# Eight heads' sample products of an mLSTM core placed on four column groups of TensorE, with their rows on 128 partitions

## What is computed

```python
S = jnp.einsum('bhtd,bhsd->bhts', qc, kc) * jnp.exp(D - mt[..., None])
wi = jnp.exp(inter - mt)
num = wi[..., None] * jnp.einsum('bhvd,bhtd->bhtv', C, qc) + jnp.einsum('bhts,bhsv->bhtv', S, vc)
den = wi * jnp.einsum('bhd,bhtd->bht', n, qc) + jnp.sum(S, axis=-1)
hc = num / jnp.maximum(jnp.abs(den), jnp.exp(-mt))[..., None]
```

## Time and profile before

| | |
|---|---|
| time, median of 3 runs | 2181.82 us (2179.68 to 2181.86) |
| the profiled execution: its own time | 2179.15 us |
| its span in the trace | 2177.4 us |
| TensorE busy | 2141.7 us, 98% |
| VectorE, ScalarE, GpSimd busy | 59%, 29%, 12% |
| mLSTM stages and output projection | 1352 to 1536 us of the span |

### The profile page before, as it was taken

How to read it: one execution, slowest core, us unless ns; L and a number is a source line. 1 busy time by engine, 2 the same in 40 slices (tenths; PEclk the granted TensorE clock), 3 DMA queues, 4 the chain that set the end, 5 groups by cost and what they waited for, 6 DMA issues and landing times.

```text
span 2177.4 us, 30006 instructions
## 1 busy us (share of the span) xinstructions
PE 2141.7 (98%) x11026; PEld 1680.8 (77%) x11026; DVE 1275.3 (59%) x2997; ACT 641.5 (29%) x1467; POOL 264.1 (12%) x499
## 2 busy tenths in 40 slices
PE   8999999999999999999999999999999999999998
PEld 7656777776878888888888775778888888888887
DVE  5215996654386776777422665443876776676223
ACT  3005885543232222221001220542322222220002
POOL 1002000000012222221000000320122222220000
PEclk9999999999999999999999999999999999999999
DMA  8135405984312232221222224132322222222223
GB/s 198 55 96 163 132 2 140 268 213 104 101 39 78 87 98 87 78 78 59 97 78 78 88 78 98 59 100 70 114 83 78 78 78 78 78 88 86 78 78 113
DMA packets 206916, 209.66 MB, mean 96 GB/s; under 512 B 40467, under 2 KB 192251, under 8 KB 206515
## 3 DMA queue, kind: packets, MB, share of 16 engines
q1 hardware_dynamic: 202754, 189.99, 30.5%
q0 software_dynamic: 4016, 17.75, 2.4%
HBM read 196.33 MB, written 19.70 MB: 99 GB/s over the span
## 4 chain that ended last, share of the span: by engine, by line
PE 95%; DVE 2%; ACT 1%; issue 1%; DMA 0%; SPq 0%; DVEq 0%; ACTq 0%
PE PS L2824 57%; PE PS L2685 4%; PE PS L768 3%; PE PS L1630 3%; PE PS L1770 2%; PE PS L2670 2%; PE PS L1525 2%; PE PS L1569 2%; PE PS L2784 2%; PE PS L697 2%; PE PS L684 2%; PE PS L717 2%; PE PS L2599 1%; PE PS L756 1%; PE PS L782 1%; PE PS L889 1%
## 5 line engine op out<-in xcount | busy, mean ns | idle before, releaser
L2824 PE MATMUL PS<-HT,ring 128*128 128x272 f32 x1536 | 374.3, 393 | 4.0 <-DVE HT L3534 4.0
L2824 PEld LDWEIGHTS PS<-HT,ring 128*128 128x128 f32 x1536 | 291.9, 190 | 65.2 <-issue 3.6
L2824 PE MATMUL PS<-arena,ring 128*128 128x272 f32 x1392 | 341.8, 392 | 0.0
L2824 PEld LDWEIGHTS PS<-arena,ring 128*128 128x128 f32 x1392 | 264.3, 190 | 54.4
L3168 ACT ACTIVATE arena<-arena,CB,CW 128x560 f32<-128x560 f32 x128 | 109.0, 853 | 377.5 <-DVE arena L3594 313.2
L2824 PE MATMUL PS<-arena,CONST 128*128 128x272 f32 x768 | 191.7, 392 | 0.0
L2824 PE MATMUL PS<-arena 128*128 128x272 f32 x768 | 191.3, 392 | 0.0
L3609 DVE SCALAR_TENSOR_TENSOR arena<-arena,CW 128x560 f32<-128x560 f32 x256 | 187.3, 790 | 0.0
L2824 PEld LDWEIGHTS PS<-arena,CONST 128*128 128x128 f32 x768 | 145.9, 190 | 30.1
L2824 PEld LDWEIGHTS PS<-arena 128*128 128x128 f32 x768 | 145.8, 190 | 30.0
L3808 POOL COPY arena<-arena 128x16 f32<-128x16 f32 x128 | 50.9, 398 | 622.9 <-DVE arena L3594 525.2
(11 more groups left out here) (517 smaller groups left out, 3359.8 us busy)
## 6 DMA issues: line engine op xcount, KB each, us to landing
ring<-in_w_ffn_up SPq DMA_DIRECT2D x64, 1024.0 KB, 6.5
ring<-in_w_ffn_down SPq DMA_DIRECT2D x32, 1024.0 KB, 5.1
ring<-in_cache_nsa_kv SPq DMA_DIRECT2D x128, 128.0 KB, 6.0
arena<-in_cache_nsa_kv SPq DMA_DIRECT2D x56, 256.0 KB, 6.4
ring<-in_w_ml_in SPq DMA_DIRECT2D x12, 1024.0 KB, 5.9
arena<-in_cache_nsa_win SPq DMA_DIRECT2D x16, 512.0 KB, 5.6
out_nsa_win_sample<-in_cache_nsa_win POOLq DMA_DIRECT2D x8, 1016.0 KB, 17.5
ring<-in_w_nsa_in SPq DMA_DIRECT2D x6, 1024.0 KB, 5.4
```

Source lines behind the costliest of these rows:

```text
L2824: last = mm(PS[:, bank, 0:HALF], lhs[:, k, :], rhs(k), start=(first and k == 0), stop=(done and k == 3))
```

## The change

In all of it head h = 4r + j gets the column group j (PSUM partitions 32j to 32j + 31) and the row r of two.

- `sample_inter()` does all 32 matmuls in stage 12, for each r and q one after the other on the four column groups, into bank 7. `sample_intra()` does its eight in stage 13, in the same way, into bank 6. Nothing of either is left in stage 15 or behind the loop.
- The results stand on 128 partitions (`SNUM`, 2 by 129 for a partition). So `sample_rows()` is two activations in stage 12, `sample_add()` one addition in VectorE's stage 13, `sample_denominators()` stands in VectorE's stage 14 with two reductions, and `sample_normed()` one multiplication, ahead of `normed_heads(3)`.
- The factors are needed per partition too: `token_columns` gains eight small matmuls (8 by 32 against 8 by 2) into bank 4, and VectorE a copy of four columns (`TKS`).
- On ScalarE the root of the sample group stands ahead of `head_root(3)`.
- `turn_pair(2)` waits for the one `sample_rows` and the one `sample_add`. `turn_pair(3)` moves from behind block m = 1 to behind block m = 2 and waits for both `sample_normed` and `normed_heads(3)`. `turn_sample` is two transposes of 128 by 128.

```diff
--- before.py
+++ after.py
@@ -390,7 +390,8 @@
 
         r_at = m_.place[0]
...
-        SQH = arena[0:SMP, r_at:r_at + 1024].rearrange("p (h v) -> p h v", h=MLH)
+        SQH = arena[:, r_at:r_at + 256].rearrange("p (r v) -> p r v", r=2)
+        SNUM = RT[:, 0:2 * (DV + 1)].rearrange("p (r v) -> p r v", r=2)
...
-        MSTS = m_(8 * 8, "p (q h) -> p q h", rows=SMP, q=8)
+        MSTS = m_(8 * 8, "p (q h) -> p q h", q=8)[:, :, 0:2]
...
+        TKS = m_(4, "p (q r) -> p q r", q=2)
...
@@ -1534,6 +1535,10 @@
...
+                for q, row in enumerate((WI, EM)):
+                    for j in range(4):
+                        mm(PS[32 * j:32 * j + 32, 4, 160 + 2 * q:162 + 2 * q], row[:, col], ident[0:8, j:8:4],
+                           start=True, stop=True)
...
@@ -1685,36 +1690,30 @@
...
-            def sample_inter(g):
-                if g == 0:
-                    pe.wait_ge(s_cn, 8)
-                    pe.wait_ge(s_qx, 1)
-                    pe.wait_ge(s_c0e, 9)
-                elif g == 1:
-                    pe.wait_ge(s_cn, 9)
-                else:
-                    pe.wait_ge(s_sne, 1)
-                bank = (7, 6, 7)[g]
-                for j, h in enumerate(INTER[g]):
+            def sample_inter():
+                pe.wait_ge(s_cn, 8)
+                pe.wait_ge(s_qx, 1)
+                pe.wait_ge(s_c0e, 9)
+                for r in range(2):
                     for q in range(4):
-                        last = mm(PS[0:SMP, bank, j * W129:(j + 1) * W129], QX[:, h, q, :], CT0[:, h, q, :],
-                                  start=(q == 0), stop=(q == 3))
+                        for j in range(4):
+                            h = 4 * r + j
+                            last = mm(PS[32 * j:32 * j + 32, 7, r * W129:(r + 1) * W129], QX[:, h, q, :], CT0[:, h, q, :],
+                                      start=(q == 0), stop=(q == 3))
                 last.then_inc(s_sn, 1)
 
-            def sample_intra(g):
-                bank = (6, 7, 4)[g]
-                if g < 2:
-                    pe.wait_ge(s_mo, 6)
-                else:
-                    pe.wait_ge(s_oe, 15)
-                for j, h in enumerate(INTER[g]):
-                    last = mm(PS[0:SMP, bank, j * W129:(j + 1) * W129], SMS[:, h, :], VA[0:SMP, 4, h, :],
-                              start=True, stop=True)
+            def sample_intra():
+                pe.wait_ge(s_cn, 9)
+                for r in range(2):
+                    for j in range(4):
+                        h = 4 * r + j
+                        last = mm(PS[32 * j:32 * j + 32, 6, r * W129:(r + 1) * W129], SMS[:, h, :], VA[0:SMP, 4, h, :],
+                                  start=True, stop=True)
                 last.then_inc(s_sn, 1)
 
             def turn_pair(n):
 
-                pe.wait_ge(s_hv, n + 1)
+                pe.wait_ge(s_hv, n + 1 if n < 3 else 5)
                 for h2 in range(2):
                     for c in range(4):
                         last = tr(PS[:, 6 + h2, c * P:(c + 1) * P], NUM[:, n % 2, c, h2, 0:DV], ident)
@@ -1746,23 +1745,19 @@
                     state_update(7)
                 elif s == 12:
                     sum_update()
-                    sample_inter(0)
+                    sample_inter()
                 elif s == 13:
-                    sample_inter(1)
-                    sample_inter(2)
+                    sample_intra()
                 elif s == 14:
-                    pe.wait_ge(s_sne, 3)
+                    pe.wait_ge(s_sne, 1)
+                    pe.wait_ge(s_sna, 1)
                     turn_pair(2)
-                elif s == 15:
-                    sample_intra(0)
-                    sample_intra(1)
 
             for u in range(16):
                 front(u)
                 gate_half(u)
                 intra(u)
                 sample_part(u)
-            sample_intra(2)
 
...
@@ -1779,9 +1774,8 @@
             def turn_sample():
                 pe.wait_ge(s_oe, 16)
                 pe.wait_ge(s_hv, 5)
-                for h in range(MLH):
-                    num = (RT, RR)[h // 4][0:SMP, (h % 4) * W129:(h % 4) * W129 + DV]
-                    last = tr(PS[:, 5, 32 * h:32 * h + 32], num, ident[0:32, 0:32])
+                for r in range(2):
+                    last = tr(PS[:, 5, r * P:(r + 1) * P], SNUM[:, r, 0:DV], ident)
                 last.then_inc(s_mt, 1)
 
             def turn_memory():
@@ -1799,8 +1793,7 @@
                 if m % 2 == 0:
                     out_arrived(m)
                 out_part(m, m, 0, range(0, 6))
-                if m == 1:
-                    pe.wait_ge(s_sna, 2)
+                if m == 2:
                     turn_pair(3)
             pe.wait_ge(s_mo, 8)
             for m in range(4):
...
@@ -1906,13 +1899,11 @@
                 else:
...
-            def sample_rows(g):
-                act.wait_ge(s_sn, g + 1)
-                bank = (7, 6, 7)[g]
-                for j, h in enumerate(INTER[g]):
-                    last = nc.scalar.activation((RT, RR)[h // 4][0:SMP, (h % 4) * W129:(h % 4 + 1) * W129],
-                                                PS[0:SMP, bank, j * W129:(j + 1) * W129], ACT.Copy,
-                                                scale=TK[0:SMP, 4, 0, h:h + 1])
+            def sample_rows():
+                act.wait_ge(s_sn, 1)
+                for r in range(2):
+                    last = nc.scalar.activation(SNUM[:, r, :], PS[:, 7, r * W129:(r + 1) * W129], ACT.Copy,
+                                                scale=TKS[:, 0, r:r + 1])
                 last.then_inc(s_sne, 1)
 
...
@@ -1954,19 +1945,16 @@
                     for j in ((0, 1), (2, 3), (4, 5, 6), (7, 8))[u - 2]:
                         state_copy(j)
                 elif u == 12:
-                    sample_rows(0)
-                elif u == 13:
-                    sample_rows(1)
-                    sample_rows(2)
+                    sample_rows()
                 if c == 0 and n:
                     head_root(n - 1)
                     open_gates(n - 1)
             open_gates(3)
             squares(15)
+            act.wait_ge(s_ms, 4)
+            nc.scalar.activation(MSTS[:, 4, :], MSTS[:, 3, :], ACT.Sqrt, bias=eps[:, 0:1], scale=1.0 / DV)\
+                .then_inc(s_mrt, 1)
             head_root(3)
-            act.wait_ge(s_ms, 5)
-            nc.scalar.activation(MSTS[:, 4, :], MSTS[:, 3, :], ACT.Sqrt, bias=eps[0:SMP, 0:1], scale=1.0 / DV)\
-                .then_inc(s_mrt, 1)
 
...
@@ -2063,6 +2051,7 @@
                 dve.wait_ge(s_tkm, 1)
...
+                v.tensor_copy(TKS.rearrange("p q r -> p (q r)"), PS[:, 4, 160:164])
...
@@ -2210,40 +2199,30 @@
                               PS[0:SMP, 6 + h2, 256:384].rearrange("p (h t) -> p h t", h=4), ALU.mult)
                 last.then_inc(s_md2, 1)
 
-            def sample_add(g):
-                dve.wait_ge(s_sn, 4 + g)
-                dve.wait_ge(s_sne, g + 1)
-                bank = (6, 7, 4)[g]
-                for j, h in enumerate(INTER[g]):
-                    num = (RT, RR)[h // 4][0:SMP, (h % 4) * W129:(h % 4 + 1) * W129]
-                    last = tt(num, num, PS[0:SMP, bank, j * W129:(j + 1) * W129], ALU.add)
-                last.then_inc(s_sna, 1)
-
-            sample_heads = [row[0:SMP, 0:4 * W129].rearrange("p (h v) -> p h v", h=4) for row in (RT, RR)]
+            def sample_add():
+                dve.wait_ge(s_sn, 2)
+                dve.wait_ge(s_sne, 1)
+                tt(SNUM, SNUM, PS[:, 6, 0:2 * W129].rearrange("p (r v) -> p r v", r=2), ALU.add).then_inc(s_sna, 1)
 
             def sample_denominators():
-                dve.wait_ge(s_sna, 3)
+                dve.wait_ge(s_sna, 1)
                 dve.wait_ge(s_cu, MLH)
-                for r, num in enumerate(sample_heads):
-                    d = num[:, :, DV]
-                    last = v.scalar_tensor_tensor(out=MSTS[:, 0, 4 * r:4 * r + 4], in0=d, scalar=-1.0, in1=d,
-                                                  op0=ALU.mult, op1=ALU.max)
-                    for h in range(4):
-                        v.tensor_tensor_reduce(out=SQH[:, 4 * r + h, :], in0=num[:, h, 0:DV], in1=num[:, h, 0:DV],
-                                               scale=1.0, scalar=0.0, op0=ALU.mult, op1=ALU.add,
-                                               accum_out=MSTS[:, 1, 4 * r + h:4 * r + h + 1]).then_inc(s_dc, 1)
-                        chain.k += 1
+                d = SNUM[:, :, DV]
+                last = v.scalar_tensor_tensor(out=MSTS[:, 0, :], in0=d, scalar=-1.0, in1=d, op0=ALU.mult, op1=ALU.max)
+                for r in range(2):
+                    v.tensor_tensor_reduce(out=SQH[:, r, :], in0=SNUM[:, r, 0:DV], in1=SNUM[:, r, 0:DV],
+                                           scale=1.0, scalar=0.0, op0=ALU.mult, op1=ALU.add,
+                                           accum_out=MSTS[:, 1, r:r + 1]).then_inc(s_dc, 1)
+                    chain.k += 1
                 chain.link(last)
```

(26 more changed lines are left out.)

## The result

The changed kernel took 2169.34 us, median of 4 runs (2166.68 to 2172.83), against 2181.22 us for the kernel before (4 runs, 2179.68 to 2181.86): a ratio of 0.9948 with a 95% interval of 0.9933 to 0.9964. The profiled execution took 2172.83 us, with a span of 2171.1 us where the kernel before had 2177.4; that is 6.3 us and not 11.9. Timed again, on one chip together with the kernel before, the changed kernel took 2172.94 us (8 runs) against 2179.2 (25 runs), a ratio of 0.9971 (0.9959 to 0.9983). So the first thing to settle is which of the two differences belongs to the change.

The account below looks back on a forecast made before the run. TensorE, busy for 98% of the span, was taken to bound the kernel. 5.4 + 1.35 - 0.45 - 0.8 + 1.15 + 0.35 = 7.0 us off the median of 2181.82 gave 2174.8 us, range 2171.5 to 2178.5.

Parts of the forecast that it names:

- products with memory: Line 1700 on TensorE, 64 records: in turn on four column groups 1.9 us instead of 7.31, gain 5.4 us.
- products among themselves: Line 1711 on TensorE: 16 records moved to stage 13 on four groups, 0.47 us instead of 1.8, gain 1.35 us.
- columns of factors: Eight added small matmuls on TensorE cost 0.45 us; the added copy on VectorE is hidden behind a wait.
- stall in stage 14: TensorE, arriving earlier at line 1615, waits for ScalarE's line 1938 behind three table loads: cost 0.8 us.
- `turn_pair(3)`: Transposes on TensorE in the projection: placed behind 36 records they no longer wait for VectorE's line 2191, gain 1.15 us.
- `turn_sample`: On TensorE, eight transposes in 0.61 us become two of 128 by 128 at 0.11 each, gain 0.35 us.
- steps costed at nothing: Waits of `turn_pair(2)`, `sample_denominators` in VectorE's stage 14, `gated(3)` and SyncE's weight loads: cost 0 each.
- Rival 1: Other engines take back more, at stage 14 and `turn_pair(3)`: stall 1.9 us, gain only 4.2 us, 2177.6 us; 6%.
- Rival 2: Column groups with their own weights overlap less in both products: gain 4.8 us at factor two, 0.25 without overlap; 7%.
- Rival 3: TensorE's clock falls behind the packed block in stage 12: costs 13 us up to `intra(15)`'s end, 2187.8 us; 3%.
- I carry the difference over to the median: Last step: the profiled execution is 2.7 us below the runs' median, so 7.0 us comes off 2181.82, giving 2174.8.
- 1 us for the spread of the median: Allowance in the forecast's lower end of 2171.5 us, beside no stall in stage 14 and the cheapest prices.

## Why the prediction was right in the trace and wrong in the time

| step | forecast | measured | from |
|---|---|---|---|
| products with memory | +5.4 | +5.36 | 7.31 to 1.95 on the chain |
| products among themselves | +1.35 | +1.51 | 1.88 and 0.20 behind them, to 0.57 |
| columns of factors | -0.45 | -0.31 | 1314.28 to 1315.42, less the 0.83 of lateness |
| stall in stage 14 | -0.8 | -0.78 | the run with the rows behind the gates |
| `turn_pair(3)` | +1.15 | +0.92 | the run with only its place changed |
| `turn_sample` | +0.35 | +0.39 | 0.61 to 0.22 |
| sum | 7.0 | 7.09; the distance gives 7.15 | |

**Right.** Every step came where it was forecast, and none is off by more than 0.23 us. (The 0.57 us of the products among themselves is a little more than the 0.5 that was given as their sign.) The steps costed at nothing were nothing: `turn_pair(2)` follows without a wait, the weights came in time, and no wait of VectorE reached TensorE. Rival 1 (the other engines take back more) did not come: the stall was 0.78 and not 1.9 us, and line 2180 ended 1.23 us ahead of `turn_pair(3)`, where 1.2 were forecast. Rival 2 (less overlap with other weights in each group) fell: 0.030 us for a record with its own weights against 0.029 at line 1557. The 3.07 of the Trainium skill, "TensorE: Matmul & The Clock Gate", section "Measured speedup vs the span model", a figure for four row tiles, would have left 3.0 us for both products; the trace has 2.5, a factor of 3.7 for line 1701. The warning of the Trainium skill, "TensorEngine Tiling (Array Packing)", section "PSUM Bottleneck", was to the point in where to look: the new wait is on the engine that empties PSUM, though on its table loads and not on the copy of 0.63 us. Rival 3 (the clock falls behind the packed block) did not come: the granted clock is 1.00 from 1300 to 2150 us in every trace.

**Wrong.** The step that failed is the last one, "I carry the difference over to the median", with its allowance of "1 us for the spread of the median". It took the three runs of before for the kernel's scatter, and let the changed kernel start from their level. What the runs showed instead: the unchanged kernel scatters over 8.7 us (2173.63 to 2182.37), and its time goes with the mean granted clock of the run, 0.994 to 0.998; three runs that agree within 2.2 us had, by the table, only fallen on neighbouring levels. A range around a gain of 7 us would have had to allow some 4 us either way for this.

The prediction also read the clock wrongly. It says that the trace shows the clock lowered once, from 25 to 30 us. The same trace has 0.83 at 120 and at 190 us and 0.88 at 610 too; its mean of 0.996 is less than one fall of 3.4 us would leave (1.7 us lost of 2177 is 0.999). I used the one fall that I had seen for a rival on the change, and did not ask what the falls meant for the comparison itself.

That the first four runs of the changed kernel missed the range was chance in which level they fell on. It is as much chance that the second time, 2172.94 us, is inside: seven of its eight runs had 0.995, a level that the times of before fit too.

## What to carry to other kernels

Where small matmuls fill 32 of the 128 columns, as the 64 records here do, put four such on the four column groups and issue them in turn, one on each (1.95 us where one group took 7.31). Two in turn already give most of it (2.47); runs of 16 records on one group give most of it away (5.97). Before taking work off the bottleneck engine, look for the engine that the work had covered, here a chain of table loads, and let that chain start first: moving one call on ScalarE gave back the 0.78 us that the change had newly lost. And compare kernels whose difference is below a per cent over a stretch between two marks in the trace, after a look at the granted clock within it: 845.93 and 853.08 us repeated to 0.01, while the times scattered by over 8 us. Three runs that agree do not show the scatter: here they lay within 2.2 us, and the kernel's is 8.7.

## What the runs showed of the hardware that I had not expected

- Matmuls on different column groups overlap over a change of group, not only in strict turn: each change saved 0.43 us, nearly four records of 0.114 us, with runs of 8 and of 16 records alike (4.33 and 5.97 us for the same 64). What limits it to 0.43 us the runs don't tell.
- The first 36 records of the projection took 0.20 us longer (8.45 against 8.25) behind 16 records on 32 rows and one column group than behind records on 128 rows. Why is open.
- The same instructions lost between 0 and 3.4 us to the lower clock at a given place (190 us) from one execution to the next. The fastest and the slowest run of an unchanged kernel, with mean granted clocks of 0.998 and 0.995, lie 8.7 us apart; where the fastest gains it no trace shows.
